# Two more filling products around the slots' ranks, and the product for the slots' table moved between the units of two experts

## The reference

```python
def hier_moe(h, w_rg, b_rg, w_re, b_re, w_gate, w_up, w_down):
    g_p, g_idx = lax.top_k(jax.nn.softmax(g_logits, axis=-1), 1)      # 1 of 4 groups
    e_top, e_idx = lax.top_k(e_logits, TOP_K_IN_GROUP)                # 2 of its 8 experts
    gate = g_p * jax.nn.softmax(e_top, axis=-1)
    ...
    def expert_block(args):
        xb, e = args
        return (jax.nn.silu(xb @ w_gate[e]) * (xb @ w_up[e])) @ w_down[e]
    y_rows = y_rows * row_w[:, None]
    out = jnp.zeros((T + 1, D)).at[row_token].add(y_rows)[:T]
```

## Time and profile before

| | us |
|---|---|
| median of 3 runs (lowest, highest) | 697.87 (697.35, 697.98) |
| the profiled execution | 697.5 |
| its span, first to last instruction | 695.6 |
| TensorE busy | 670.1 (96%) |
| VectorE, ScalarE, GpSimd busy | 355.5, 295.0, 149.1 |
| bytes moved by DMA | 181.46 MB, 261 GB/s over the span |

### The profile page before, as it was taken

The page is one execution under the profiler, slowest core; times in us unless marked ns, Lnnn a source line. Parts: engine busy times, 40 slices in busy tenths (PEclk is TensorE's granted clock), DMA queues, the critical chain, the costliest instruction groups (busy, mean ns, idle before and its releaser), DMA issues.

```text
span 695.6 us, 12108 instructions
## 1 busy us (share of the span) xinstructions
PE 670.1 (96%) x4941; PEld 541.2 (78%) x4941; DVE 355.5 (51%) x579; ACT 295.0 (42%) x486; POOL 149.1 (21%) x148
## 2 busy tenths in 40 slices
PE   6999999999999999999999999998899999999984
PEld 5998886999999999977999999985555555555532
DVE  6359544666666666568555564676222323232313
ACT  5244556454444444455574544334113222322223
POOL 0586865033333333322004000000000000000000
PEclk9999999999999999999999999999789999999999
DMA  8961334555555555542443349888699999999994
GB/s 343 423 255 60 123 106 175 212 193 196 191 193 188 181 181 181 182 179 71 175 164 140 139 165 375 329 339 349 239 412 421 420 420 421 421 420 421 420 421 191
DMA packets 25681, 181.46 MB, mean 261 GB/s; under 512 B 2848, under 2 KB 3104, under 8 KB 4128
## 3 DMA queue, kind: packets, MB, share of 16 engines
q1 hardware_dynamic: 25488, 180.69, 66.6%
q10 hardware_dynamic: 144, 0.07, 0.1%
HBM read 179.70 MB, written 1.05 MB: 260 GB/s over the span
## 4 chain that ended last, share of the span: by engine, by line
PE 85%; DMA 4%; DVE 4%; POOL 2%; ACT 2%; issue 1%; SPq 0%; POOLq 0%; ACTq 0%; DVEq 0%
PE psum L682 50%; PE psum L1287 8%; PE psum L1270 4%; PE psum L1311 4%; PE psum L1294 4%; DMA ring<-units_in 4%; PE psum L1303 4%; PE psum L669 1%; PE psum L645 1%; DVE ffn_w_low L531 1%; DVE arena L2256 1%; PE psum L1028 1%; POOL first_odd L1927 1%; DMA const<-const_in 1%; PE psum L721 1%
## 5 line engine op out<-in xcount | busy, mean ns | idle before, releaser
L531 DVE TENSOR_TENSOR ffn_w_low<-ring,ffn_w_high 128x2048 fp32r<-128x2048 f32 x55 | 131.2, 2386 | 111.0 <-ACT ffn_w_high L526 110.8
L526 ACT ACTIVATE ffn_w_high<-ring 128x2048 fp32r<-128x2048 f32 x56 | 107.4, 1918 | 141.2 <-PE psum L682 141.1
L682 PE MATMUL psum<-ht_high,ffn_w_high 128*128 128x256 f32 x552 | 156.8, 284 | 0.8 <-DVE ffn_w_low L531 0.8
L682 PE MATMUL psum<-ht_low,ffn_w_high 128*128 128x256 f32 x552 | 156.2, 283 | 0.0
L682 PE MATMUL psum<-ht_high,ffn_w_low 128*128 128x256 f32 x552 | 156.2, 283 | 0.0
L682 PEld LDWEIGHTS psum<-ht_high,ffn_w_high 128*128 128x128 f32 x552 | 105.9, 192 | 2.5 <-DVE ffn_w_low L531 1.2
L682 PEld LDWEIGHTS psum<-ht_low,ffn_w_high 128*128 128x128 f32 x552 | 105.9, 192 | 0.3
L682 PEld LDWEIGHTS psum<-ht_high,ffn_w_low 128*128 128x128 f32 x552 | 105.9, 192 | 0.0
L2573 DVE SCALAR_TENSOR_TENSOR weighted<-psum,arena,weighted 128x512 fp32r<-128x512 f32 x31 | 23.3, 751 | 70.3 <-ACT weighted L1813 70.3
L1964 POOL TENSOR_TENSOR arena<-arena 128x512 f32<-128x512 f32 x10 | 28.6, 2864 | 119.3 <-ACT arena L1657 96.9
L1791 ACT ACTIVATE arena<-psum,arena 128x512 f32<-128x512 f32 x32 | 22.0, 687 | 61.1 <-PE psum L1287 53.6
(11 more groups left out here) (398 smaller groups left out, 1296.5 us busy)
## 6 DMA issues: line engine op xcount, KB each, us to landing
ring<-units_in SPq DMA_DIRECT2D x94, 1024.0 KB, 5.0
arena<-units_in SPq DMA_DIRECT2D x29, 1024.0 KB, 22.0
spare_units<-units_in SPq DMA_DIRECT2D x10, 1024.0 KB, 15.6
small_units<-units_in SPq DMA_DIRECT2D x10, 1024.0 KB, 16.9
early_unit<-units_in SPq DMA_DIRECT2D x5, 1024.0 KB, 17.0
HN<-units_in SPq DMA_DIRECT2D x5, 1024.0 KB, 18.7
rows<-units_in SPq DMA_DIRECT2D x4, 1024.0 KB, 17.2
features_unit<-units_in SPq DMA_DIRECT2D x4, 1024.0 KB, 20.9
```

Source lines behind the costliest of these rows:

```text
L526: nc.scalar.activation(parts_slot(n)[0], w, ACT.Copy).then_inc(hi_ready, 1)
L531: nc.vector.tensor_tensor(l, ring[:, n % RING, :], h.bitcast(fp32), SUB).then_inc(lo_ready, 1)
L682: last = mm(o, l[a], r[b], start=start and (a, b) == pairs[0], stop=stop and (a, b) == pairs[-1])
```

## The change

A second filling product, of 256 columns, stands behind the one between `residual` and the wait for `m_ready`; a third, of 384 columns, behind the rank products. The wait for `table_in` and the table's product move from behind the four units of experts 0 and 1 to between those of expert 0 and those of expert 1.

```diff
             residual(1).then_inc(x_summed, 1)
             stay_busy(1, 2, c_("iota"))
+            stay_busy(1, 2, c_("iota"), 256)
             pe.wait_ge(m_ready, 1)
...
             last.then_inc(rank_done, 1)
+            stay_busy(1, 2, c_("iota"), 384)
...
             expert_up(tokens_for(0), unit(pe, U_EXP + 1), range(HALF_K, KD), FIRST_BANK).then_inc(unit_used, 1)
+            pe.wait_ge(table_in, 1)
+            table(TABLE_BANK, 0).then_inc(table_done, 1)
             for g in range(2):
                 expert_up(tokens_for(1), unit(pe, gate_of(1) + g), range(g * HALF_K, (g + 1) * HALF_K)
                           ).then_inc(unit_used, 1)
-            pe.wait_ge(table_in, 1)
-            table(TABLE_BANK, 0).then_inc(table_done, 1)
             pe.wait_ge(table_sb, 1)
```

## The result

The changed kernel takes 693.18 us (median of 4 executions, 692.44 to 693.27) against 697.92 us for the kernel before beside it (4 executions, 697.35 to 698.98): 0.9927 of it, 95% interval 0.9911 to 0.9943, 4.7 us less. I had forecast 3.5 us less, 694.4 us, with 692.9 us as the lower end. 0.9927 of the 697.87 us from which I forecast is 692.8 us, just outside. Direction and mechanism came out as said; the gain was undersized by a quarter.

A forecast was written before the change was run, and what follows sets the result against it. The late restart of the transfer queue was taken to set the end. 0 + 0 - 2.85 - 0.45 = -3.3 us gave 694.2 us from the profile, 694.6 from the median; forecast 694.4 us, range 692.9 to 697.3 us.

The forecast's parts named there:

- What sets the end: Expert loop: the moment the queue of transfers restarts, and how full it stays after that, set the end.
- The fillers cost nothing: Around the rank products: both filling products hide in TensorE's idleness, 0 us; bounds for the second 0 and +0.2 us.
- The clock holds: From 486 us on, the fillers keep TensorE at full clock; 695.6 to 692.9 us, chance 0.72.
- a clock of 0.50 anywhere from 486 to 510 us: Sign of a wrong forecast: granted clock was to be 1.00 in every stretch there.
- The path to the first slot: Gathering and expert 0's first unit at full clock free the first slot earlier: -2.85 us, bounds 2.5 and 3.1.
- The table: Ahead of expert 1's units: 0.6 us wait for VectorE, two slots freed later at no cost, fold at about 496 us.
- The queue behind the start: DMA from 509 to 513 us: shortfall behind the late issue at 507.06 us goes, -0.45 us, bounds 0 and 1.5.
- the hole at 499 us: DMA shortfall with four transfers outstanding, expected again; together with the start itself some 1.0 us.
- the second fall: Clock drop between 502 and 504 us: expected to go, moving only TensorE, which is ahead of the transfers anyway.
- The fillers don't do it: Rival: the clock falls at the same point while gathering; 697.3 us, between 696.9 and 697.8, chance 0.17.
- The fall is only put off: Rival: the clock falls at about 492 us, at the table's wait and narrow products; 696.1 us, chance 0.08.
- The rule of the Trainium skill: Mid-kernel clock drops need idle gaps far longer than 0.88, 0.78 and 1.28 us, so filling them changes nothing here.

The follow-up runs named there:

- the filler of 256 alone: Kernel before plus only the filling product of 256 columns in front of the rank products; 697.08 us.
- the table alone: Kernel before with only the table's wait and product moved ahead of expert 1's units, no filling product added; 696.82 us, 0.9991 of before.
- the unit ahead of the third group: Changed kernel with expert 0's first unit used ahead of the third group of gathered features; 692.69 us with two further fillers, 692.86 us without.
- the second issue late: Changed kernel with the expert loop's second transfer issued only when the third unit has been used; 694.09 us.
- the fillers alone: Kernel before plus only the two filling products, the table staying behind expert 1's units; 694.55 us, 0.9946 of before.

## What of the prediction was right, and which step failed

*What sets the end: right.* The start of the queue of transfers does, and not TensorE's chain, although the chain of waits names TensorE for most of the stretch. Delaying the first issue by 0.86 us cost 0.75 us; taking 17 us of products away gave 0.2 us.

*The fillers cost nothing: right.* TensorE still idles 0.43 us in front of the ranks, the margin that I gave, and gathering starts 0.06 us behind VectorE's `batch_onehot`. Even twice the second filler made the path to the first issue only 0.35 us longer.

*The clock holds: right where it matters, not throughout.* In both profiled executions of the changed kernel it holds while gathering and up to the first freed slot, and the times of all 15 agree with that. But I had named a clock of 0.50 anywhere from 486 to 510 us as a sign of being wrong, and one of the two profiles shows it from 499.7 to 503.1 us, at no cost. What I did not see either is that the kernel before varies too: by time and mean clock, one of its executions in ten escapes the fall. A forecast from one profile took the common case for the only one.

*The path to the first slot, -2.85 us: it measured -2.72 us.* Gathering took 3.81 us up to the next step where I had about 3.7.

*The table: right in each step.* It waits 0.51 us for VectorE (0.6 expected), expert 1's products cover the copying, and the fold starts at 495.46 us in a profile in which everything stands 0.7 us earlier (about 496 expected). That the two slots freed later would cost nothing held: the DMA engines moved 422 GB/s from 494 us on.

*The queue behind the start, -0.45 us: this is the step that failed, in its size.* It measured -1.54 us in the profile, beyond even my outer bound of 1.5 us; with the path it makes 4.26 us where I had 3.3. I had counted the 1.49 us that the rows are short of the full rate, and took only the part behind the late sixth issue, in the belief that the hole at 499 us with several transfers outstanding would come again. It didn't: the same 17 us behind the first issue have 412 GB/s in the changed kernel, so only 0.4 us of the 1.49 is left. The two parts that are gone can be priced from the kernel before:

```profile
498.65:500.65 2.00, 0.71 (x8) 0.62 (x6) 0.32 (x2) 0.69 (x1) 0.00 (x0) 1.00 0.96 303
500.65:502.65 2.00, 1.27 (x13) 0.53 (x12) 0.49 (x2) 0.80 (x2) 0.00 (x0) 0.94 1.00 393
508.65:510.65 2.00, 2.00 (x20) 0.70 (x12) 0.00 (x0) 1.37 (x2) 0.00 (x0) 0.86 1.04 369
510.65:512.65 2.00, 2.00 (x20) 1.26 (x20) 0.97 (x2) 0.22 (x1) 0.00 (x0) 1.00 0.97 389
```

Against 421 GB/s the first pair, 4 to 8 us behind the first issue, is 0.7 us short, and the second pair, 14 to 18 us behind it, 0.4 us; the changed kernel has neither. The second is the term that I took. The first is the one that I left out, and it is the larger.

What goes with it is the distance of the second issue from the first. The kernels in which that is 1.4 us or more (before, the filler of 256 alone, the table alone, the unit ahead of the third group with and without fillers, the second issue late) all have a stretch of 2 us with 193 to 356 GB/s in these 4 us. The others, with 0.86 us or less, have none below 414. In the kernel before the distance is 1.42 us because expert 0's second unit too was used at 1.2 GHz. Delays of single issues show that such holes cost time, though only for larger ones: the second issue at 3.5 us costs B 1.5 us, the sixth at 14.0 us 1.7 us. Why 0.56 us between two issues empties the engines 4 us later, with four transfers outstanding, is not shown.

So what I wrote of the second fall, that it only moves TensorE, which is ahead anyway, doesn't hold where TensorE isn't ahead yet. From 502.4 us to the sixth issue at 507.06 us the kernel before ran at half speed, which is some 2.3 of the 3.2 us by which that issue comes later than in the changed kernel (an estimate from the clock and the two times). With the fillers alone the fall took 2.36 us of B back.

*The rivals.* "The fillers don't do it" is what the filler of 256 alone looks like (697.08 us). "The fall is only put off" came true in the kernel with the fillers alone, though in front of the fold and not of the table, and in a harmless form in one execution of the changed kernel. The rule of the Trainium skill (TensorE: Matmul & The Clock Gate, "Why this matters for your kernels") that a drop in mid-kernel needs much longer gaps would have given 697.3 us. This case does not bear it out: with the fillers alone the clock fell at about 496.8 us, inside the eight short products behind a gap of 1.29 us.

## What to carry to other kernels

Where transfers set the end, look for the moment at which their queue restarts, and ask which products of the path to it run at the low clock: a filling product in an idle gap ahead of that path can be worth several times its own length (here 3.3 us by the medians, for some 1.1 us of products). Keep the first few issues close behind each other: what the DMA engines miss there is never made up, as the 20 us behind the first issue show (353 to 391 GB/s from kernel to kernel, then 419 to 422 in all of them). And look at the granted clock of every execution, not only of the profiled one, before taking a fall of the clock (or its absence) for a property of the program.

## What I had not expected of the hardware

A queue that restarts empty loses time twice. The first transfer of 1 MB moves only 86 GB/s in the 2 us behind its issue at 491.56 us, and then alone keeps the engines at 418 GB/s. But if the next is issued only 3.5 us behind it, the engines fall to 184 GB/s for 2 us while it starts up in turn. With the second 0.86 us behind the first, the changed kernel has 422 GB/s from 494 to 496 us.

The moment at which the clock falls or rises isn't fixed to the program. The same kernel ran with a mean clock of 0.983 to 0.990 in 75 executions and 0.992 to 0.995 in 8, and its time followed: 696.35 to 700.07 us against 693.05 to 693.57 us.
